# RWKV stage of a two-block model: two gating units go from the stage's end to the front of its first pair, and the weight tile of the units is reloaded after the fourth level

## The reference, cut to what matters

```python
z = h @ w_in[l]
zu, zv, zr = jnp.split(z, [GMLP_WIDTH, 2 * GMLP_WIDTH], axis=-1)
y_a = _gmlp_mixer(zu, zv, ...)      # gelu(zu) * (causal mix over chunks of the normed gelu(zv))
y_b = _rwkv7_mixer(zr, ...)
...
# the scan inside _rwkv7_mixer, per head and token
sa = jnp.einsum('bhvk,bhk->bhv', state, a_t)
state = state * w_t[:, :, None, :] + sa[..., None] * b_t[:, :, None, :] + v_t[..., None] * k_t[:, :, None, :]
y_t = jnp.einsum('bhvk,bhk->bhv', state, r_t)
```

## Time and profile before

| | |
|---|---|
| median of 3 runs | 3020.45 us (3018.6 to 3021.95) |
| profiled execution, its own time | 3012.71 us |
| span in the profile | 3011.0 us |
| mean granted TensorE clock | 0.985 |
| TensorE (PE) busy | 2877.3 us |
| VectorE (DVE) busy | 1754.4 us |
| ScalarE (ACT) busy | 1247.9 us |
| GpSimd (POOL) busy | 460.4 us |
| `stage_rwkv_pairs` | from 1527.5 us to the barrier's end at 2094.2 us |

### The profile page before, as it was taken

One profiled execution on the slowest core, in us unless ns is written; L12 is line 12 of the kernel. 1 busy time (PEld: TensorE's weight loads), 2 busy tenths in 40 slices (PEclk: granted clock), 3 DMA queues, 4 the chain that ended last, 5 costly groups with the idle time before them and its releaser, 6 DMA issues. The chain is left out here.

```text
span 3011.0 us, 47785 instructions
## 1 busy us (share of the span) xinstructions
PE 2877.3 (96%) x19568; PEld 2186.5 (73%) x19568; DVE 1754.4 (58%) x2519; ACT 1247.9 (41%) x2016; POOL 460.4 (15%) x354
## 2 busy tenths in 40 slices
PE   8999999999999999998999999999799899999996
PEld 6877744677777777776756677688688787777784
DVE  2332223486566666666426535262885899999995
ACT  2111100023455555543222213132443788888883
POOL 2222100031222222213131010110000100000002
PEclk9999999999999999999999999999799999999998
DMA  5111031573211111121121122012663899999997
GB/s 171 46 39 39 21 133 56 162 225 119 63 57 57 57 57 57 57 102 67 67 65 34 34 64 65 11 60 88 229 231 140 316 399 399 399 400 400 400 375 279
DMA packets 290957, 454.44 MB, mean 151 GB/s; under 512 B 15776, under 2 KB 157600, under 8 KB 290768
## 3 DMA queue, kind: packets, MB, share of 16 engines
q1 hardware_dynamic: 283712, 426.06, 40.5%
q0 software_dynamic: 7056, 25.69, 2.3%
HBM read 389.77 MB, written 61.93 MB: 150 GB/s over the span
## 5 line engine op out<-in xcount | busy, mean ns | idle before, releaser
L1019 PE MATMUL psum<-x_hi,w_hi 128*128 128x512 f32 x512 | 210.7, 412 | 2.3 <-PEq L100 1.6
L1212 DVE TENSOR_TENSOR fox_pT_lo<-psum,fox_pT_hi 128x512 fp32r<-128x512 f32 (+2 forms) x192 | 107.2, 558 | 180.4 <-ACT fox_pT_hi L1151 171.0
L1021 PE MATMUL psum<-x_hi,w_lo 128*128 128x512 f32 x512 | 201.0, 393 | 0.0
L1020 PE MATMUL psum<-x_lo,w_hi 128*128 128x512 f32 x512 | 199.9, 390 | 0.0
L724 PE MATMUL psum<-wo,yT 128*128 128x512 f32 x384 | 167.9, 593 | 2.9 <-PEq L100 1.5
L1711 PE MATMUL psum<-hT,wr 128*128 128x512 f32 x384 | 167.1, 593 | 0.0
L3188 DVE TENSOR_TENSOR lo_g<-land_g,hi_g 128x2048 fp32r<-128x2048 f32 x66 | 148.3, 2289 | 18.4 <-ACT hi_g L3114 18.4
L3188 DVE TENSOR_TENSOR lo_u<-land_u,hi_u 128x2048 fp32r<-128x2048 f32 x66 | 150.5, 2283 | 0.0
L1162 ACT ACTIVATE fox_p<-fox_p,fox_bias 128x256 f32<-128x256 f32 (+7 forms) x128 | 99.7, 779 | 117.8 <-DVE fox_bias L1198 113.9
L3188 DVE TENSOR_TENSOR lo_d<-land_d,hi_d 128x2048 fp32r<-128x2048 f32 x66 | 148.1, 2285 | 0.7 <-ACT hi_d L3114 0.7
L3114 ACT CAST hi_d<-land_d 128x2048 fp32r<-128x2048 f32 x66 | 125.8, 1910 | 45.3 <-DMA land_d<-in_moe_w_down 34.3
(11 more groups left out here) (543 smaller groups left out, 7256.7 us busy)
## 6 DMA issues: line engine op xcount, KB each, us to landing
land_g<-in_moe_w_gate SPq DMA_DIRECT2D x66, 1024.0 KB, 11.2
land_u<-in_moe_w_up SPq DMA_DIRECT2D x66, 1024.0 KB, 12.4
land_d<-in_moe_w_down SPq DMA_DIRECT2D x66, 1024.0 KB, 12.7
ada<-in_ada_w SPq DMA_DIRECT2D x24, 1024.0 KB
y_slots<-yb SPq DMA_DIRECT2D x33, 512.0 KB, 13.7
w<-in_w_in SPq DMA_DIRECT2D x27, 512.0 KB, 4.1
w_land<-in_w_kv_shared SPq DMA_DIRECT2D x23, 512.0 KB, 4.1
w_land<-in_w_in SPq DMA_DIRECT2D x23, 512.0 KB, 4.0
```

The costliest lines, as they stand in the source:

```text
L1019: nc.tensor.matmul(bank[:], hi[:, d, :], E.x_hi[:, d, cols], start=(d == 0), stop=False)
L1020: nc.tensor.matmul(bank[:], hi[:, d, :], E.x_lo[:, d, cols], start=False, stop=False)
L1021: last = nc.tensor.matmul(bank[:], lo[:, d, :], E.x_hi[:, d, cols], start=False, stop=(d == ND - 1))
L1212: V.tensor_tensor(pT_lo[j][:, s0:s1, half], ringT.bank(("t", n, j, s0))[:, 0:(s1 - s0) * P].rearrange("p (s n) -> p s n", n=P), pT_hi[j][: ...
```

## The change

Two units leave the place `("Yi", 3)` and two are added to `("first", 0)`.

```diff
-        fill = {("small", 0): 1, ("first", 0): 3}
+        fill = {("small", 0): 1, ("first", 0): 5}
         for c in range(NPAIR):
             fill |= {("X", c): 1, ("ak", c): 1, ("GH", c): 1, ("N", c): 1}
             if c > 0:
                 fill |= {("level", c, 3): 1, ("level", c, 4): 1}
-                fill |= {("Yi", c): 2} if c == NPAIR - 1 else {("rk", c): 1, ("level", c, 2): 1}
+                fill |= {} if c == NPAIR - 1 else {("rk", c): 1, ("level", c, 2): 1}
```

## The result

The changed kernel is slower: 3026.82 us in the median of 18 runs (3020.89 to 3033.39), against 3016.91 us (3012.29 to 3021.95) for the kernel before in 18 runs beside them. The ratio is 1.0034, with a 95% interval of 1.0027 to 1.0041, so +10.2 us (8.1 to 12.4); the two medians themselves lie 9.9 us apart. The forecast was 3026.0 us, but as +5.5 us on the three runs then known; their median, 3020.45, lay 3.5 us above that of the 18. The time lies in the stated range, and only 0.8 us from the forecast, but that is luck: a start 3.5 us too high made up for most of a difference that is nearly twice the forecast's.

A forecast was written before the change was run, and what follows sets the result against it. TensorE, busy 2877.3 of 3011.0 us, was taken as the bound, with SyncE's stores deciding the stage's end. 6.9 - 1.4 = +5.5 us on 3020.45 gave 3026.0 us, range 3022.5 to 3029.5.

The forecast's parts named there:

- the waits marked "issue": TensorE waits ahead of pairs 1 and 2, 1.94 us together: no change taken; rival that they go, chance 0.12.
- the front: Two units added ahead of v's transposes cost 6.9 us, hidden by nothing; rival that they are free, chance 0.04.
- the end: Two units removed behind the last product: last stored byte and restart come 1.4 us earlier, at most 1.9.
- the reload at GH: Moved w_uv reload, first used at GH of pairs 1 and 2: 6.5 us slack, no cost; rival wait, chance 0.03.
- the cold start: Rival at the next stage's restart: idle TensorE drops its clock, idle-work batches run slow, 3027.5 to 3029.1 us; chance 0.15.
- my three signs of being wrong: Stage slips under 6.9 us, restart over 1.9 us closer to last product, or later stages change by over 2 us.
- Place: Theory made after the result: "issue" waits hang on where TensorE's 16 KB instruction blocks begin among dense 64x64 matmuls.
- Collision: Theory made after the result: the 1 MB w_uv reload at ak of pair 0 delays an instruction fetch.
- Work: Theory made after the result: the moved units themselves cost more at the front than the sum says.

The follow-up runs named there:

- e2: Changed kernel with 48 tiny matmuls (192 instructions) ahead of the RWKV stage and 16 (64 instructions) behind: ratio 1.0048 to the kernel before, stretch 474.8 us.
- e11: Kernel before with 64 instructions fewer ahead of the stage and 64 more behind, at the same time on TensorE: ratio 1.0005, stretch 473.9 us.
- e10: Kernel before with 128 instructions more ahead of the stage and 128 fewer behind, at the same time on TensorE: ratio 1.0022, stretch 480.1 us.
- e6: Kernel before with 64 instructions more ahead of the stage and 64 fewer behind, by exchanged idle-work matmuls, no unit moved: ratio 1.0008, stretch 476.1 us.
- e7: Changed kernel with 64 instructions fewer ahead of the stage and 64 more behind its last product: ratio 1.0023 to the kernel before, stretch 472.8 us.
- e3: Changed kernel with the first w_uv reload moved to the projection of r of pair 1, issued only some 0.6 us later: ratio 1.0036, stretch 476.2 us.
- e12: Changed kernel with the first w_uv reload held until r of pair 1 has left TensorE: ratio 1.0033 to the kernel before, stretch 476.1 us.
- e8: e7 with the first w_uv reload also issued at the projection of r of pair 1: ratio 1.0023 to the kernel before, stretch 473.6 us.
- e4: Against the kernel before, the two units go behind levels 3 and 4 of pair 0 instead of the front: ratio 1.0035, stretch 486.4 us.
- e5: Kernel before run once more, unchanged: ratio 0.9996, stretch 473.2 us (469.5 in its first profile).
- e9: Changed kernel run once more, unchanged: ratio 1.0034 to the kernel before, stretch 479.7 us (479.9 in its first profile).

## Why the prediction was right and wrong

The terms for the moved work came out as summed. The term for the waits marked "issue", put at no change, did not, and the start was 3.5 us too high; the two nearly cancel in the time, by luck.

**Right: the front.** From the first projection to the first transpose of v it is 65.8 us in every kernel with the five units and 58.9 in the others: 6.9 us.

**Right: the end.** 10.8 us became 9.2: 1.6 us given back where I took 1.4. The arrays' stores decide, not TensorE, which is done 6.7 us before the restart.

**Right: the reload at GH.** In pair 1 the unit at GH starts in the row behind its neighbour with no idle time, order in time on PE:

```profile
1864.68 1.96 PE L1816 MATMUL psum<-aAV,XT 64*64 64x128 f32 x32
1866.79 3.69 PE L1760 MATMUL psum<-w_uv,hT 128*128 128x256 f32 x16
```

**Right: the cold start costs nothing.** Stretches around the restart, columns as in the earlier trace rows, and the copy that the earlier trace rows had:

```profile
2112.00:2116.00 4.00, 0.00 (x0) 0.00 (x0) 0.00 (x0) 0.00 (x0) 0.00 (x0) 0.67 0.60 186
2116.00:2120.00 4.00, 3.82 (x18) 3.85 (x19) 0.70 (x2) 1.28 (x1) 0.31 (x1) 0.50 0.61 159
2120.00:2124.00 4.00, 4.00 (x46) 3.81 (x46) 0.85 (x2) 0.56 (x2) 0.00 (x0) 0.98 1.02 274
...
2131.61 0.63 ACT L2551 ACTIVATE gu<-s_uv 128x512 f32<-128x512 f32 x1 [2.39 <-DMA s_uv<-uv_rows_dram]
```

The clock did fall to 0.50, the 1.2 GHz level, during the 6.7 us without work. It was back while the batches ran, TensorE's wait for GpSimd ahead of ws shrank from 2.11 to 0.32 us, and the gelu of the second tile came 15.5 us behind the restart (15.3 before), still waiting for data. From the restart to the first cast of the experts' weights (`L3114`) it is 220.1 us in both profiles.

**Wrong: "I take no change and keep both ends" for the waits marked "issue".** This was the failed step. I had seen that they hang on the place in the instruction stream and that two units' instructions now stand ahead of the pairs, and then treated the result as a toss between -1.94 and +1.27. Measured, the two large groups sum to 8.5 us, and all waits of this kind over 0.25 us to 9.7 in both profiles of the changed kernel, against 2.7 and 5.0 before. With 6.9 - 1.6 = 5.3 us for the moved work, 4.9 us of the 10.2 (2.8 to 7.1) are left for them and the clock behind them. None of my three signs of being wrong would have caught it: I asked whether the stage slips by less than 6.9 us, and from its first projection to its last product it slipped by 17.3 us in the first profiles and 13.4 in the second.

*Place* is shown in the traces. The stretch grows from 469.5 and 473.2 us to 476.1 by a shift of 64 instructions without any moved work, with waits at the changed kernel's own matmuls, and shrinks by 7 us when the changed kernel is shifted back. In 12 of 14 profiles pair 0 has a wait behind 7686 or 7687 recorded matmuls of the program, whichever product stands there, and those of e2 and e11 stand on the same grid: the borders are fixed and the change moved the work across them. In the time, +128 is slower than before beyond its interval (e10). The share in the change is less sure: 2.4 us by e6 (-0.3 to 4.8) and 3.3 us by e7 against the changed kernel, where the two intervals overlap, and nothing by e2.

*Collision* is shown for one wait: 3.08 to 3.44 us in the four profiles in which the unit at ak issues the reload ahead of its store, 0.21 to 1.15 in the eight others that stop there. The packets show how: counted from the matmul 126 places ahead of the stop, the block's packet starts 3.4 to 3.9 us later in those four and 0.5 to 1.7 us later in the eight, while its transfer takes 0.9 to 1.7 us in all of them. I had written that the reload at ak "has level 1 to 5 ahead of it" and looked only at its user, not at what else the transfer delays. That it costs 2.3 us of the whole time is not shown: e3, e12 and e8 removed the long wait and had ratios within 0.0002 of the kernels that they start from, with intervals of 3 to 4 us to each side. The profiled executions of e3 and e12 were the fastest of their runs, so their stretches may flatter them. How much of the 1.6 to 2.5 us that place leaves open is the reload, and how much chance in the lengths of the other waits, stays open.

*Work* fell with e4.

The chances gave 0.43 to slower by over 0.2%, and by the sum's own terms this was the wrong side of an even case: the two ends of the "issue" term were not alike. The kernel before had two large waits in its stage, and its other profile (e5) shows 2.2 us more of such waits than the one that I had read; of the three other places tried on it, +64 and +128 were worse in the stretch and -64 was like it. So a new place is more likely to be worse than better.

## What to carry to other kernels

A move of work on an engine with a long unrolled stream of short instructions also moves every later instruction against the fetch blocks. Take the "issue" waits of before as one draw of several, look whether they are few, and expect the average of other places, not the same sum again. When a bulk load is issued at a new moment, look at what is fetched in the dense part that follows, not only at who needs the load. And where a difference of 0.2% is at stake, shift the stream by instructions that cost no time before blaming the edit.

## What the runs showed of the hardware

The page lists 140 packets with 2.29 MB on the queue of kind "instruction", 16 KB each. The Trainium skill, "Runtime: NRT & Kernel Launch", section "Instruction fetch mechanics", says that an engine's memory for instructions is refilled in blocks of 16 KiB, or 256 instructions, and that the cost of crossing a border is mostly hidden, since instructions are dispatched more slowly than they are refilled. The size agrees, and so does the grid: 126.8 recorded matmuls with their weight loads are 254 recorded instructions. That it is hidden does not hold in this stage: at 128 recorded instructions in about 1 us of 64x64 matmuls, TensorE stopped for up to 1.8 us at such places with no bulk transfer near (0 to 44 GB/s in the 3 us ahead of the packet).

In the six waits of over 2.4 us the packet itself started only after TensorE had stopped, with 264 to 343 GB/s moving: the four at AV, and two at pair 2 (2.75 us in e5, 2.43 in e8), where the pair's four arrays were being stored. So it is not only the reload of `w_uv` that can do this. Nor does bulk traffic always do it: 17 of the waits, of 0.5 to 1.6 us, had 333 to 388 GB/s ahead of their packet. What makes the difference is not shown.

Such a stop can also cost the clock. Seven of the 14 profiles have 3.4 us at 0.50 at the end of or just behind a stop of 1.6 to 3.2 us, at most 1.7 us each time, while e7 and e9 kept the full clock through 3.08 and 3.44 us. In the changed kernel the granted clock around the end of the 3.17 us wait was 0.57 over 4 us, after a stretch with 1.56 us of work in 4:

```profile
1645.00:1649.00 4.00, 1.56 (x79) 1.43 (x72) 2.07 (x4) 0.00 (x0) 4.00 (x4) 1.00 0.85 274
1649.00:1653.00 4.00, 3.27 (x69) 3.27 (x70) 0.00 (x0) 1.17 (x2) 1.51 (x2) 0.57 0.04 8
```
